# Order of work at the seam between the delta rule's scan and the output projection of the even layer

## What is computed

```
def even_mixer(h, w_in, w_out, ...):
    rq, rk, rv, rg, gq, gk, gv, gg, ga, gb = _split(h @ w_in, EVEN_SPLITS)
    ...
    ret = rmsnorm(o_f + flip(o_b), ret_norm_w).transpose(0, 2, 1, 3).reshape(b, t, RET_V)
    ret = ret * jax.nn.silu(rg)
    ...
    od_f, sg_f = chunk_gated_delta_rule(q, k, v, g[0], beta[0], s0_gdn[:, 0])
    od_b, sg_b = chunk_gated_delta_rule(flip(q), flip(k), flip(v), jnp.flip(g[1], axis=-1), ...)
    gdn = rmsnorm(od_f + flip(od_b), gdn_norm_w).transpose(0, 2, 1, 3).reshape(b, t, GDN_V)
    gdn = gdn * jax.nn.silu(gg)
    out = jnp.concatenate([ret, gdn], axis=-1) @ w_out
```

## Time and profile before

| | us |
|---|---|
| median of 3 runs | 2717.14 |
| lowest and highest of them | 2715.86, 2717.32 |
| the profiled execution | 2716.23 |
| its span, first to last instruction | 2714.4 |
| PE busy | 2628.3 (97%) |
| VectorE busy | 1621.0 (60%) |
| ScalarE busy | 881.3 (32%) |
| GpSimd busy | 285.9 (11%) |

### The profile page before, as it was taken

How to read it: one execution, slowest core, us unless ns; L and a number is a source line. 1 busy time by engine, 2 the same in 40 slices (tenths; PEclk the granted TensorE clock), 3 DMA queues, 4 the chain that set the end, 5 groups by cost and what they waited for, 6 DMA issues and landing times.

```text
span 2714.4 us, 47492 instructions
## 1 busy us (share of the span) xinstructions
PE 2628.3 (97%) x18589; PEld 2536.8 (93%) x18589; DVE 1621.0 (60%) x2548; ACT 881.3 (32%) x1441; POOL 285.9 (11%) x244
## 2 busy tenths in 40 slices
PE   7999999999979899999999999999989999999998
PEld 6999999999948799999999999999967799999998
DVE  5797776726585678877765724425667763322335
ACT  5222122523324352221244212124446644221223
POOL 0000000300001310000021000003145530000002
PEclk9999999999999899999999999999989999999999
DMA  8464454321012345544543423224110042222222
GB/s 272 132 182 150 132 152 136 114 78 63 26 41 60 109 133 159 158 155 136 159 124 92 126 78 124 73 67 149 64 58 2 1 130 65 85 77 78 78 76 102
DMA packets 353374, 284.67 MB, mean 105 GB/s; under 512 B 30908, under 2 KB 313656, under 8 KB 353240
## 3 DMA queue, kind: packets, MB, share of 16 engines
q1 hardware_dynamic: 350616, 282.51, 34.4%
q10 hardware_dynamic: 2624, 0.33, 0.1%
HBM read 275.85 MB, written 4.98 MB: 103 GB/s over the span
## 4 chain that ended last, share of the span: by engine, by line
PE 88%; DVE 6%; issue 3%; ACT 1%; DMA 1%; SPq 0%; POOL 0%; DVEq 0%; ACTq 0%; POOLq 0%
PE ps L344 79%; PE ps L2371 1%; PE ps L2358 1%; PE ps L2348 1%; DVE mod_acc L404 1%; PE ps L2349 1%; DVE step L1585 1%; DVE x L795 1%; DVE w_lo L325 1%; DVE a_neg L2456 0%; DVE blocks L1589 0%; DVE pt L2469 0%; DVE mod_t L416 0%; PE ps L2127 0%; DMA x_tok<-in_x_sample_dram 0%
## 5 line engine op out<-in xcount | busy, mean ns | idle before, releaser
L344 PE MATMUL ps<-h_hi,w_hi 128*128 128x320 f32 x3712 | 1154.4, 311 | 5.9 <-DVE h_lo L528 4.2
L344 PE MATMUL ps<-h_hi,w_lo 128*128 128x320 f32 x3712 | 1148.2, 309 | 0.0
L344 PE MATMUL ps<-h_lo,w_hi 128*128 128x320 f32 x3712 | 1148.1, 309 | 0.0
L344 PEld LDWEIGHTS ps<-h_hi,w_hi 128*128 128x128 f32 x3712 | 698.0, 188 | 14.6 <-issue 8.9
L344 PEld LDWEIGHTS ps<-h_lo,w_hi 128*128 128x128 f32 x3712 | 697.9, 188 | 1.0 <-issue 0.5
L344 PEld LDWEIGHTS ps<-h_hi,w_lo 128*128 128x128 f32 x3712 | 697.7, 188 | 0.0
L316 ACT CAST w_hi<-w_raw 128x1024 fp32r<-128x1024 f32 x376 | 374.6, 1046 | 591.3 <-PE ps L344 572.1
L325 DVE TENSOR_TENSOR w_lo<-w_raw,w_hi 128x1024 fp32r<-128x1024 f32 x376 | 453.2, 1247 | 12.8 <-ACT w_hi L316 7.5
L344 PE MATMUL ps<-hid_hi,w_hi 128*128 128x320 f32 x1408 | 437.0, 310 | 0.0
L344 PE MATMUL ps<-hid_hi,w_lo 128*128 128x320 f32 x1408 | 435.1, 309 | 0.0
L344 PE MATMUL ps<-hid_lo,w_hi 128*128 128x320 f32 x1408 | 435.1, 309 | 0.0
(11 more groups left out here) (295 smaller groups left out, 2028.3 us busy)
## 6 DMA issues: line engine op xcount, KB each, us to landing
w_raw<-in_ffn_w_in_dram SPq DMA_DIRECT2D x176, 512.0 KB, 5.3
mod_raw<-in_mod_w_dram SPq DMA_DIRECT2D x64, 1024.0 KB, 5.2
w_raw<-in_ffn_w_out_dram SPq DMA_DIRECT2D x96, 512.0 KB, 4.4
w_raw<-in_even_w_in_dram SPq DMA_DIRECT2D x28, 512.0 KB, 4.3
w_raw<-in_ffn_w_out_dram SPq DMA_DIRECT2D x32, 384.0 KB, 5.5
mod_first<-in_mod_w_dram SPq DMA_DIRECT2D x4, 2048.0 KB, 14.7
w_raw<-in_even_w_out_dram SPq DMA_DIRECT2D x16, 512.0 KB, 4.3
w_raw<-in_odd_w_out_dram SPq DMA_DIRECT2D x16, 512.0 KB, 4.3
```

The source lines that it names most:

```text
L344: mm = nc.tensor.matmul(ps[:, 4 * s + 2 * n + b, 0:HALF], w[s][:, k, cols], v[:, k, b * HALF:(b + 1) * HALF], start=(first and k == 0), st ...
```

## The change

The parts, as the code has them:

- The retention's four mixed tiles are split during the scan. ScalarE makes their high parts in steps 1 and 2 (two tiles in each), GpSimd their low parts ahead of its own share of steps 3 and 4. The high parts go to the place of the retention's gate (`proj_r` from RG0), the low parts over the tiles themselves (`proj_r` from RV0), not to `h_hi` and `h_lo`, whose room the scan uses.
- PE no longer does the five turns in one place. The turn of the first tile stands inside step 4, ahead of its output products; those of tiles 3, 2 and 1 stand behind the first 24 products of the even output (slab 0, k 0 to 3); that of tile 4 stands behind the first pair of groups. The first pair is split by k: slab 0 with k 0 to 3, three turns, slab 1 with k 0 to 3, then k 4 to 7 of either slab.
- In step 4 the backward unit comes first, so tile 1 is complete ahead of tile 4, and `O_ORDER` is 0, 3, 2, 1, 4. The first 320 tokens need tiles 0, 1 and half of 2 alone.
- The delta rule's four mixed tiles are split in two halves of 320 tokens: the first behind the fourth turned tile, the second (`act_mixed_late`, `dve_mixed_late`) behind the first two groups' adds.
- GpSimd squares tiles 3 and 2 within step 3 and scales tile 0 ahead of its adds of step 4. The turns use other banks.
- The loops over even output's groups are written out for the first body.

```
-            for m in range(2):
+            for m in parts:
 ...
+        def pe_even_first(pe):
+            g = GROUPS["even_out"]
+            def steps(s, k0, k1):
+                pe.wait_ge(wlo_ready, 2 * (g + s) + 1 + k0 // 4)
+                for k in range(k0, k1):
+                    pe.wait_ge(mo_lo, k + 1)
+                    mm = pe_half_step(pe, s, k, 0, mixed_hi, mixed_lo, k == KT - 1)
+                return mm
+            pe.wait_ge(group_out, g)
+            steps(0, 0, 4)
+            for i in (1, 2, 3):
+                pe_o_turn(pe, i)
+            steps(1, 0, 4)
+            steps(0, 4, KT).then_inc(group_mm, 1)
+            steps(1, 4, KT).then_inc(group_mm, 1)
+            pe_o_turn(pe, 4)
 ...
+                if t == 4:
+                    pe.wait_ge(y_ready, 10)
+                    pe_o_turn(pe, 0)
-                for d, q, n in units(t):
+                for d, q, n in units(t) if t < 4 else units(t)[::-1]:
 ...
-            for i, n in enumerate(O_ORDER):
-                if i < 3:
-                    pe.wait_ge(o_norm, i + 1)
-                else:
-                    pe.wait_ge(o_late, i - 2)
-                if i >= 2:
-                    pe.wait_ge(mo_full, i - 1)
 ...
+                if t in (1, 2):
+                    for j in (2 * t - 2, 2 * t - 1):
+                        act.wait_ge(tn_out, 8 + j + 1)
+                        nc.scalar.copy(proj_r[:, RG0 + j, :], proj[:, RV0 + j, :]).then_inc(mo_hi, 1)
                 if t == 3:
                     act.wait_ge(oo_mm, 6)
                     act_split(act, GROUPS["even_out"], 0)
-            for i in range(3):
+                    act_o_root(act, 0)
+            for i in (1, 2):
                 act_o_root(act, i)
+            act.wait_ge(oo_mm, 10)
+            act_split(act, GROUPS["even_out"] + 1, 1, (0,))
+            act_o_root(act, 3)
+            act_split(act, GROUPS["even_out"] + 1, 1, (1,))
             act.wait_ge(out_done, 48)
+            act.wait_ge(mo_full, 4)
             for j in range(4):
-                act_mixed_high(act, j, RV0 + j)
+                if j == 3:
+                    act.wait_ge(o_added, 10)
+                nc.scalar.copy(h_hi[:, 4 + j, 0:HALF], proj[:, GV0 + j, 0:HALF]).then_inc(mo_hi, 1)
+            act_o_root(act, 4)
 ...
+        mixed_hi = ((proj_r, RG0), (h_hi, 0))
+        mixed_lo = ((proj_r, RV0), (h_lo, 0))
-        O_ORDER = (0, 3, 2, 4, 1)
+        O_ORDER = (0, 3, 2, 1, 4)
 ...
+                    if t == 4 and d == 1:
+                        dve_o_out(dve, 0)
+                        for i in (1, 2):
+                            dve_o_rec(dve, i)
+                        o_square(dve, nc.vector, 3)
+                        dve_o_sum(dve, 3)
+                        dve_o_rec(dve, 3)
+                        o_scale(dve, nc.vector, 3, o_late)
+                        dve_split(dve, GROUPS["even_out"] + 1, 1, (0,))
+                        for i in (1, 2, 3):
+                            dve_o_out(dve, i)
 ...
         def pool_scan(pool):
+            for j in range(4):
+                pool.wait_ge(mo_hi, j + 1)
+                nc.gpsimd.tensor_tensor(proj_r[:, RV0 + j, :], proj[:, RV0 + j, :], proj_r[:, RG0 + j, :].bitcast(F32), ALU.subtract
+                                        ).then_inc(mo_lo, 1)
 ...
```

More of the change, by code:

```diff
@@ L304, in body_loop, with act_split @@
                 body(i)
-        def act_split(act, g, s):
+        def act_split(act, g, s, parts=(0, 1)):
             if isinstance(g, int) and g >= NGROUPS:
@@ L313, in act_split, with dve_split @@
                 act.wait_ge(group_mm, g - 1)
-            for m in range(2):
+            for m in parts:
                 k = slice(4 * m, 4 * m + 4)
                 nc.scalar.copy(w_hi[s][:, k, :], w_raw[s][:, k, :]).then_inc(whi_ready, 1)
-        def dve_split(dve, g, s):
+        def dve_split(dve, g, s, parts=(0, 1)):
             if isinstance(g, int) and g >= NGROUPS:
                 return
-            for m in range(2):
+            for m in parts:
                 k = slice(4 * m, 4 * m + 4)
@@ L870, in pe_ffn, with act_linear @@
             pe_late_half(pe, NORM_AFTER[name], GROUPS[name] + LOOPS[-1][2], FFN_CHUNKS[-1], hid_hi, hid_lo)
-        def act_linear(act, name, groups):
+        def act_linear(act, name, groups, late=None):
             def body(i):
@@ L880, in body @@
                         act_squares(act, 2 * NORM_AFTER[name], GROUPS[name] + 2 * i + s, 2 * i + s)
-            body_loop(act, GROUPS[name], groups // 2, body)
+                if late is not None and isinstance(i, int) and i == 0:
+                    late(act)
+            body_loop(act, GROUPS[name], groups // 2, body, first=int(late is not None), peel=int(late is not None))
             if name in NORM_AFTER:
@@ L898, in pe_linear_in, with pe_linear_out, dve_add_groups @@
             body_loop(pe, GROUPS[name], groups // 2, body, first=static)
-        def pe_linear_out(pe, name, ready):
+        def pe_linear_out(pe, name, hi, lo, first=None):
             def body(i):
+                if first is not None and isinstance(i, int) and i == 0:
+                    first(pe)
+                    return
                 for s in range(2):
-                    pe_group(pe, GROUPS[name] + 2 * i + s, s, KT, h_hi, h_lo, ready, halves=(0,))
-            body_loop(pe, GROUPS[name], 2, body)
-            pe_late_half(pe, NORM_AFTER[name], GROUPS[name] + 4, KT, h_hi, h_lo)
-        def dve_add_groups(dve, name, groups, k):
+                    pe_group(pe, GROUPS[name] + 2 * i + s, s, KT, hi, lo, None, halves=(0,))
+            body_loop(pe, GROUPS[name], 2, body, first=int(first is not None))
+            if first is not None:
+                pe.wait_ge(mo_late, 4)
+            pe_late_half(pe, NORM_AFTER[name], GROUPS[name] + 4, KT, hi, lo)
+        def pe_even_first(pe):
[14 more added lines that the diff above has]
+            pe_o_turn(pe, 4)
+        def dve_add_groups(dve, name, groups, k, late=None):
             def body(i):
@@ L914, in body @@
                     dve_split(dve, GROUPS[name] + 2 * i + s + 2, s)
-            body_loop(dve, GROUPS[name], groups // 2, body)
+                if late is not None and isinstance(i, int) and i == 0:
+                    late(dve)
+            body_loop(dve, GROUPS[name], groups // 2, body, first=int(late is not None), peel=int(late is not None))
             a, layer, j = NEXT[name]
@@ L1916, in pool_scan, with dve_mixed_late @@
+            for j in range(4):
+                dve_mixed_low(dve, j, False)
+            dve_split(dve, GROUPS["even_out"] + 1, 1, (1,))
+            o_square(dve, nc.vector, 4)
+            dve_o_sum(dve, 4)
+            dve_gate(dve, 1, 0, 1, 1.0, 12)
+            dve_o_rec(dve, 4)
+            o_scale(dve, nc.vector, 4, o_late)
+        def dve_mixed_late(dve):
+            dve_o_out(dve, 4)
+            for j in range(4):
+                dve_mixed_low(dve, j, True)
         def pool_scan(pool):
+            for j in range(4):
+                pool.wait_ge(mo_hi, j + 1)
+                nc.gpsimd.tensor_tensor(proj_r[:, RV0 + j, :], proj[:, RV0 + j, :], proj_r[:, RG0 + j, :].bitcast(F32), ALU.subtract
+                                        ).then_inc(mo_lo, 1)
@@ L1923, in pool_scan @@
                     o_square(pool, nc.gpsimd, 0)
+                    for i in (1, 2):
+                        o_square(pool, nc.gpsimd, i)
+                    o_scale(pool, nc.gpsimd, 0, o_norm)
             for i in (1, 2):
-                o_square(pool, nc.gpsimd, i)
-            for i in range(3):
                 o_scale(pool, nc.gpsimd, i, o_norm)
@@ L1938, in act_even @@
             act_scan(act)
-            act_linear(act, "even_out", 4)
+            act_linear(act, "even_out", 4, act_mixed_late)
         def dve_even(dve):
```

80 lines of the change are left out of this document (37 added, 43 removed).

## The result

| | before | after |
|---|---|---|
| median of 6 runs each, us | 2717.02 | 2701.33 |
| lowest and highest, us | 2715.86, 2717.53 | 2699.60, 2702.82 |
| the profiled execution, us | 2716.23 | 2699.90 |
| its span, us | 2714.4 | 2697.9 |

The ratio is 0.9941, with a 95% interval from 0.9931 to 0.9951: faster by 0.59%, or 15.7 us. The forecast was 14.6 us less, 2702.5; the median lies 1.2 us under it and inside the range. The page's chain of waits still goes over PE (89% of the span; 88% in the earlier trace rows).

The account below looks back on a forecast made before the run. PE bounds the kernel, held at the seam by a chain over other engines. Output products 2.05, groups 28.04, pickup 0.4, turns 2.6, pauses 0.9 + 1.3 make 35.3 us against 49.89: 14.6 less, median 2702.5; range 2700.5 to 2707.

Parts of the forecast that it names:

- pauses: PE's waits at the seam: 0.9 us ahead of tile 0's turn, 1.3 us around the three turns and slab 1.
- groups and rest: Even output's first four groups at 7.01 us each, 28.04 us, plus 0.4 us until VectorE picks up the last.
- the lock rival: VectorE and GpSimd take turns by whole instructions: scales 0.9 us, not 1.6; 0.8 us less, 2701.7; chance 0.25.
- the bound of 15.9: Most that could be saved at the seam, 15.9 us, as pauses can't be under 0.9 us.
- The turns and the clock: PE's turns at granted clock 1.00: 20 transposes in 2.6 us, slow first products (0.7 us) gone too.
- tile 2's scale: GpSimd's scale, 1.6 us stretched, ready at 890.0, holding PE 0.8 us ahead of tile 2's turn.
- The first turn: Tile 0's turn in step 4 waits for both `gdn_y`, delayed by tile 0's root, to 882.66: 0.9 us pause.
- Slab 1's first part: VectorE's first `w_lo` part of slab 1, ready at 891.5 behind tile 1's scale; PE waits 0.5 us.
- The two thin covers: VectorE ahead of PE by 0.3 us at tile 4's first low part, 0.2 at the third slab's; no pause charged.
- the rival in which VectorE's chain becomes the bound: From scan's end to the third slab, late scales or thin covers add 2 to 5 us: 2706; chance 0.15.
- It doesn't do what it says: One late tile among the three turns holds the pair; pauses of 9 to 12 us return: 2713; chance 0.05.
- Slower: GpSimd's fp32r low parts delay the scan; at 8.7 us each the gain is gone, at 10.5 2724; chance 0.03.

Follow-up runs that it names:

- e2: Kernel before with 72 and 26 idle products put into PE's two long pauses ahead of turns; 2722.96 us, ratio 1.0022.
- e7: Kernel before with fewer idle products, 36 and 13, in PE's two long pauses ahead of turns; 2715.60 us, ratio 0.9993.
- e3: Changed kernel with the turns of tiles 3, 2 and 1 ahead of slab 0's first 24 products; 2706.06 us, ratio to before 0.9961.
- e4: Changed kernel with tile 4 finished and turned ahead of slab 1's first products; 2707.68 us, ratio to before 0.9966.
- e6: Changed kernel with a VectorE tile sum between slab 0's two low parts in step 4; 2700.73 us, ratio to before 0.9938.
- e8: Changed kernel with slab 0's second low part made by GpSimd behind its three scales, not by VectorE; 2700.30 us.
- e1: Kernel before with only the retention's tiles split during the scan, turns left in one place; 2713.79 us, ratio 0.9988.

## Why the prediction was right, point by point

**The sum.** From the end of the scan's `gdn_r` products (881.81, which is the turn's 882.53 less its pause) to the fourth add the changed kernel takes 33.99 us; the forecast had 35.3. By its terms:

| term | forecast | measured |
|---|---|---|
| pauses | 0.9 + 1.3 = 2.2 | 0.72 + 0.47 = 1.19 |
| output products | 2.05 | 1.70 (883.00 to 884.70) |
| turns | 2.6 | 0.47 + 1.64 + 0.35 = 2.46 |
| groups and rest | 28.04 + 0.4 = 28.44 | 3.61 + 10.67 + 14.36 = 28.64 |
| sum | 35.3 | 33.99 |

Measured times go from the start of one piece to the start of the next, less the pause between them, since recorded times overlap what follows. The forecast took the output products from their recorded 2.05 us, which made them 0.35 too long.

Whether the forecast or the lock rival came can't be told by the time. The forecast's 2702.5 and the lock rival's 2701.7 are 0.8 us apart, and two medians of the changed kernel, 2701.33 and 2699.81, are 1.5 apart. The rows below decide. The stretch's 15.89 us also equal the bound of 15.9 that the prediction gave for the least pauses, and that is luck: the pauses were 1.19 us in sum, not 0.9, the first of them was under that 0.9 (0.72), and the shorter output products made up the rest.

**The turns and the clock.** Right: 1.00 throughout. e2 and e7 show at the same place that the clock alone makes the difference. e3 and e4 show pauses that were too long, 2.88 and 3.94 us; one of 1.86 us in e4 was not.

**The pauses** are the term that is off most, 1.0 us too much. The step that was mis-sized is tile 2's scale, for which 0.8 us was charged. I let GpSimd and VectorE stretch each other 1.8 times, 1.6 us a scale. The two scales took 2.46 us together, 1.23 each, and the turn at 888.31 did not wait. They began at 886.22 while VectorE's square (886.12, two inputs) ran until 886.78; from there to their end they took 1.90 us, 0.95 each. VectorE's scale started at 888.08, GpSimd's last one ended at 888.68 (886.22 + 2.46), and VectorE's ended 0.55 us behind that, at 889.23: the 1.15 us are a wait for a whole instruction and then the work, not slower work. The lock rival (0.9 us a scale, no pause for tile 2, 2701.7 us) described this better than the forecast did. The rule of the Trainium skill that I had set beside it (SBUF — State Buffer, section Who interferes with whom: an exclusive lock for the whole instruction, between a VectorE instruction with two SBUF inputs and a GpSimd one that reads SBUF) agrees with these rows, and e6 with it: there GpSimd's scale and VectorE's second low part, which stands behind a sum of one input, are each late by what the other's instruction had left. VectorE's and GpSimd's timelines of e6:

```profile
880.26 1.19 DVE L326 TENSOR_TENSOR w_lo<-w_raw,w_hi 128x1024 fp32r<-128x1024 f32 x1
881.37 0.68 DVE L1885 TENSOR_REDUCE o_ss<-o_squares 128x4 f32<-128x512 f32 x1
881.96 1.47 DVE L326 TENSOR_TENSOR w_lo<-w_raw,w_hi 128x1024 fp32r<-128x1024 f32 x1
```
```profile
880.42 1.93 POOL L1902 TENSOR_TENSOR o_tok<-o_tok,o_rs 128x512 f32<-128x512 f32 x1 [2.87 <-DVE o_rs L1890]
```

The scale ends at 882.35 (880.42 + 1.93), 0.9 us behind the first low part's end; the second low part ends 1.1 us behind that, at 883.43.

**The first turn** waits for `gdn_y`, as said, 0.72 us in place of 0.9: the root of tile 0 came ahead of `gdn_qs` (878.97), where ScalarE had time, and not directly ahead of `gdn_y`. GpSimd's scale of tile 0 has little to spare behind it: it ended at 882.39 (880.46 + 1.93), where 882.1 was forecast, and `gdn_y` at 882.43. In e4, where it came late, it became what the turn waited for.

**Slab 1's first part** was forecast to hold PE for 0.5 us and held it for 0.47, though both sides of that wait came about 1 us earlier than worked out; that the size agrees is in part luck. e8 shows that it is VectorE's chain that it waits for.

**The two thin covers** held. The third slab's `w_lo` pair begins at 899.43 and PE did not wait for it. So the rival in which VectorE's chain becomes the bound did not come, though the chain of waits over 879 to 890 does run over VectorE from one row to the next.

**It doesn't do what it says** would have needed one late tile: e4 is such a case, and even it keeps 8.6 us (51.83 less 43.21) of the gain.

**Slower** needed GpSimd's fp32r pieces to take 8.7 us each. They take 1.53.

**Which part is worth what.** In the stretch: the early split alone 3.7 us (e1); taking back the turns' place costs 3.75 (e3), taking back the fifth tile's place 7.3 (e4, 1.1 of it the lock's order). These add up to 14.7 of 15.9, but they were not measured in one scheme (one added to before, two taken from after), so the remainder is not a part of its own. The turn of tile 0 inside step 4, the changed order of units and tiles, and the halves of the delta rule's tiles have no run of their own; what each of them is worth is not shown.

## What to carry to other kernels

Where the matrix engine waits for a chain over other engines, look for products that are ready early and split them so that they stand inside the chain's waits: a long pause was paid twice here, once as waiting and once as transposes and products at half clock behind it, and both went together. When two engines share a lock, price the meeting as one whole instruction of the other, not as a common slowdown. Before explaining a spread of 2 us at the place that was changed, measure that place by its own start and end; the two profiles compared here had parted ahead of it.
